# Five RMS norms summed in column groups with a later total, the forget column added with the mask, and a first solve level by transpose

## What is computed

```python
def rmsnorm(x, g):
    y = xf * lax.rsqrt(jnp.mean(xf * xf, axis=-1, keepdims=True) + EPS)
    return (y * g.astype(jnp.float32)).astype(x.dtype)
...
def fox_attention(q, k, v, logf):
    c = jnp.cumsum(logf, axis=1).transpose(0, 2, 1)
        s = (jnp.einsum("bhqd,bhkd->bhqk", qh[:, :, lo:hi], kh[:, :, :hi]).astype(jnp.float32) * scale
             + (c[:, :, lo:hi, None] - c[:, :, None, :hi]))
        mask = jnp.arange(hi)[None, :] <= jnp.arange(lo, hi)[:, None]
        p = jax.nn.softmax(jnp.where(mask, s, -jnp.inf), axis=-1).astype(vh.dtype)
...
def gated_delta_rule(q, k, v, g, beta):
    sol = lax.linalg.triangular_solve(a_mat, rhs, left_side=True, lower=True)
```

## Time and profile before

| what | value |
|---|---|
| median of 3 runs | 1651.2 us (1650.48 to 1651.35) |
| profiled execution | 1650.75 us, its span 1649.0 us |
| PE busy | 1345.0 us, 82% of the span |
| DVE, ACT busy | 643.2 us (39%), 489.4 us (30%) |
| DMA | 517.93 MB, mean 314 GB/s |
| chain of waits | PE 45%, DMA 42%, DVE 8%, ACT 3% |

### The profile page before, as it was taken

One profiled execution on the slowest core, in us unless ns is written; L12 is line 12 of the kernel. 1 busy time (PEld: TensorE's weight loads), 2 busy tenths in 40 slices (PEclk: granted clock), 3 DMA queues, 4 the chain that ended last, 5 costly groups with the idle time before them and its releaser, 6 DMA issues.

```text
span 1649.0 us, 32820 instructions
## 1 busy us (share of the span) xinstructions
PE 1345.0 (82%) x14402; PEld 1069.4 (65%) x14402; DVE 643.2 (39%) x1008; ACT 489.4 (30%) x819; POOL 0.2 (0%) x4
## 2 busy tenths in 40 slices
PE   9999999999999999998875766676576676668556
PEld 8898899999999999995543433343343343334333
DVE  7787736878887778652110101100010110111001
ACT  6765477456644555531100000000000000000001
POOL 0000000000000000000000000000000000000000
PEclk9999999999999999999998988988898899899889
DMA  8432033553556665489999999999999999999997
GB/s 321 161 128 103 26 129 106 180 201 128 194 179 231 259 226 196 156 350 387 429 428 433 430 427 428 432 430 425 433 426 430 433 429 428 428 430 431 428 432 312
DMA packets 41401, 517.93 MB, mean 314 GB/s; under 512 B 4720, under 2 KB 4848, under 8 KB 6384
## 3 DMA queue, kind: packets, MB, share of 16 engines
q1 hardware_dynamic: 41184, 516.71, 76.5%
q10 hardware_dynamic: 144, 0.17, 0.0%
HBM read 515.81 MB, written 1.05 MB: 313 GB/s over the span
## 4 chain that ended last, share of the span: by engine, by line
PE 45%; DMA 42%; DVE 8%; ACT 3%; issue 1%; SPq 1%; another core or an unknown queue 0%; DVEq 0%; ACTq 0%; PEldq 0%
DMA e_gu<-experts 41%; PE psum L323 9%; PE psum L324 9%; PE psum L325 9%; PE psum L894 7%; PE psum L935 3%; DVE w_low L1562 2%; DVE all_sq L1516 1%; PE psum L385 1%; PE psum L544 1%; ACT w_high L1008 1%; DMA w_raw<-dense 1%; PE psum L941 1%; PE psum L905 0%; DVE a_gdn_qk L1607 0%
## 5 line engine op out<-in xcount | busy, mean ns | idle before, releaser
L894 PE MATMUL psum<-e_gu,x_xt 128*32 128x256 f32 x3072 | 217.2, 446 | 177.9 <-DMA e_gu<-experts 177.8
L894 PEld LDWEIGHTS psum<-e_gu,x_xt 128*32 128x32 f32 x3072 | 108.3, 128 | 279.7 <-DMA e_gu<-experts 188.9
L323 PE MATMUL psum<-h_high,w_high 128*128 128x256 f32 x896 | 254.6, 284 | 2.6 <-DVE w_low L1562 2.6
L324 PE MATMUL psum<-h_low,w_high 128*128 128x256 f32 x896 | 251.7, 281 | 0.0
L325 PE MATMUL psum<-h_high,w_low 128*128 128x256 f32 x896 | 251.6, 281 | 0.0
L1562 DVE TENSOR_TENSOR w_low<-w_raw,w_high 128x2048 fp32r<-128x2048 f32 x100 | 228.4, 2288 | 46.5 <-ACT w_high L1008 41.6
L1008 ACT ACTIVATE w_high<-w_raw 128x2048 fp32r<-128x2048 f32 x100 | 191.2, 1914 | 64.8 <-PE psum L325 53.1
L2213 DVE COPY x_yb<-psum 128x256 f32<-128x256 f32 x64 | 27.2, 425 | 427.3 <-PE psum L935 427.3
L323 PEld LDWEIGHTS psum<-h_high,w_high 128*128 128x128 f32 x896 | 168.8, 188 | 3.7 <-DVE w_low L1562 3.2
L324 PEld LDWEIGHTS psum<-h_low,w_high 128*128 128x128 f32 x896 | 168.9, 188 | 0.4 <-issue 0.2
L325 PEld LDWEIGHTS psum<-h_high,w_low 128*128 128x128 f32 x896 | 168.8, 188 | 0.0
(11 more groups left out here) (447 smaller groups left out, 2145.4 us busy)
## 6 DMA issues: line engine op xcount, KB each, us to landing
e_gu<-experts SPq DMA_DIRECT2D x44, 4096.0 KB, 53.0
w_raw<-dense SPq DMA_DIRECT2D x100, 1024.0 KB, 4.8
e_dn<-experts SPq DMA_DIRECT2D x46, 2048.0 KB, 49.4
e_dn<-experts SPq DMA_DIRECT2D x36, 1024.0 KB, 54.8
e_gu_lo<-experts SPq DMA_DIRECT2D x16, 2048.0 KB, 51.5
e_gu_hi<-experts SPq DMA_DIRECT2D x16, 2048.0 KB, 55.9
e_gu<-experts SPq DMA_DIRECT2D x8, 1024.0 KB, 8.1
e_gu<-experts SPq DMA_DIRECT2D x2, 2560.0 KB, 10.3
```

What stands on the lines that cost most here:

```text
L323: mm(ps, w[0], src[0], start=start, stop=False, **kw)
L324: mm(ps, w[0], src[1], start=False, stop=False, **kw)
L894: last = mm(half(psum[32 * s:32 * s + 32, GU_BANK[j % 2], 0:256], P), X["xt"][:, k, CAP * j:CAP * (j + 1)], expert_gu(j, k)[:, :, s * P:(s ...
```

## The change

The five norms mix, mem, xq, ffn and n1 sum in two steps. `group_sums` makes eight products with 32 columns of ones; chunk k goes to the column group k mod 4, so that two chunks are added in each quarter of a bank's partitions. ScalarE copies the result to `sq[:, 1, :]` (`keep_sums`). `total` sums the copy over all partitions with one full-width product by ones into the other half of the bank, and ScalarE takes the root with the scale 1/(32 x 1024) (`mean_root`). For mix the total follows the group sums at once; for mem, xq and n1 it stands in the middle of the next unit; for ffn behind the rest of U0. On ScalarE the high parts of weights change places with the root: in mix three of them go behind it, and in xq and n1 one does.

The product that added c of the query goes; `tok_c` turns c into a column for each head instead (two products behind fv1, copied by VectorE), and VectorE adds column and mask in one instruction for each block of queries. Level 0 of the solve uses TensorE's transpose.

```diff
-            def mean_square(name, first=0, last=DC):
...
-                    ins = mm(ps[:, 0:T], C("inv1024"), sq[:, k, :], start=(k == 0), stop=(k == DC - 1))
...
+            def group_sums(name):
+
+                ps = aux.fill(pe, f"ms_{name}")
+                for k in range(DC):
+                    pe.wait_ge(sem("squares"), quarter(name, k // 2))
+                    g = 32 * (k % 4)
+                    ins = mm(ps[g:g + 32, 0:T], C("ones", n=32), sq[:, k, :], start=(k < 4), stop=(k >= 4))
+                ins.then_inc(sem("group_sums"), 1)
+
+            def total(name):
+
+                pe.wait_ge(sem("group_sums_kept"), NORMS.index(name) + 1)
+                ps = psum[:, aux.banks[aux.units[f"ms_{name}"] % len(aux.banks)], :]
+                aux.filled(mm(ps[:, T:2 * T], C("ones", n=P), sq[:, 1, :], start=True, stop=True), f"ms_{name}")
...
-            mean_square("mix")
+            group_sums("mix")
+            total("mix")
...
+            def tok_c():
+
+                ps = aux.fill(pe, "tok_c")
+                for t in range(TT):
+                    last = mm(ps[:, t * H:(t + 1) * H], A["rows"][0:H, 3, t * P:(t + 1) * P], ident[0:H, 0:H],
+                              start=True, stop=True)
+                aux.filled(last, "tok_c")
...
+            pe.wait_ge(sem("fox_c"), 1)
+            tok_c()
             head_sums("fss_q", "fox_sq", lambda hd: sq[:, hd, :], T)
...
-                    mm(o, C("negsel", H, hd * P, P), cs[:, 0:n], start=False, stop=False)
-                    last = mm(o, cs[:, t * P:(t + 1) * P], C("sel", H, hd * 256, n), start=False, stop=True)
+                    last = mm(o, C("negsel", H, hd * P, P), cs[:, 0:n], start=False, stop=True)
...
+                    if lv == 0:
+                        last = nc.tensor.transpose(o, A["lm"][:, un, :], ident)
...
-            mean_square("mem")
-            unit("out10", mixed); unit("out11", mixed)
+            group_sums("mem")
+            unit("out10", mixed, between=lambda: total("mem")); unit("out11", mixed)
             unit("mk0", hm, split_input("mem"))
-            mean_square("xq")
-            unit("mk1", hm)
+            group_sums("xq")
+            unit("mk1", hm, between=lambda: total("xq"))
...
                 proj.filled(last, f"up{c}")
+                if c == 0:
+                    total("ffn")
...
-            mean_square("n1")
-            unit("q21", r_gained)
+            group_sums("n1")
+            unit("q21", r_gained, between=lambda: total("n1"))
...
             squares("mix", x, lambda q: (sem(f"x_loaded{q // 2}"), 16))
+            keep_sums("mix")
+            act.wait_ge(sem("consts_loaded"), 16)
+            mean_root("mix")
             ahead(UNITS[0], 2)
-            act.wait_ge(sem("consts_loaded"), 16)
-            root("ms_mix", sq[:, 0, :])
             ahead(UNITS[0], 3)
...
             warm(ACT.Sqrt)
-            root("ms_mem", sq[:, 0, :])
+            keep_sums("mem")
             ahead("out01")
+            mean_root("mem")
...
             warm(ACT.Sqrt)
-            root("ms_ffn", sq[:, 0, :])
+            keep_sums("ffn")
+            mean_root("ffn")
...
+            warm(ACT.Sqrt)
             turn_raw("q", 0)
+            keep_sums("n1")
+            mean_root("n1")
             ahead("q20")
-            warm(ACT.Sqrt)
-            root("ms_n1", sq[:, 0, :])
...
+            ps = aux.wait(dve, "tok_c")
+            aux.emptied(V.tensor_copy(A["tok"][:, :, 20:24], half(ps[:, 0:8], 4)), "tok_c")
             lows("sq1")
...
-                link(V.tensor_copy(s, ps[:, 0:n]) if mask is None else V.tensor_tensor(s, ps[:, 0:n], mask, ALU.add))
+                for t, (lo, w) in enumerate(spans):
+                    c = slice(lo, lo + w)
+                    last = V.scalar_tensor_tensor(s[:, c], ps[:, c], row(t), mask[:, c], ALU.add, ALU.add)
+                link(last)
```

More of the change, by code:

```diff
@@ L341, in chunk_ready, with unit @@
                     pe.wait_ge(sem(ready[0]), seen[0])
-            def unit(name, src=HI, ready=None, order=range(DC), by_chunk=False):
+            def unit(name, src=HI, ready=None, order=range(DC), by_chunk=False, between=None):
                 w, seen = parts(name, DC), [0]
@@ L347, in unit @@
                 for k, i in [(k, i) for k in order for i in range(2)] if by_chunk else [(k, i) for i in range(2) for k in order]:
+                    if between and (k, i) == (order[0], 1):
+                        between()
                     chunk_ready(ready, k, seen)
@@ L378, in unit_o @@
                 done[name] = proj.full(f"{tile}{u}")
-            def mean_square(name, first=0, last=DC):
-                ps = aux.fill(pe, f"ms_{name}") if first == 0 else psum[:, 4 + aux.units[f"ms_{name}"] % 4, :]
-                for k in range(first, last):
+            def group_sums(name):
+                ps = aux.fill(pe, f"ms_{name}")
+                for k in range(DC):
                     pe.wait_ge(sem("squares"), quarter(name, k // 2))
-                    ins = mm(ps[:, 0:T], C("inv1024"), sq[:, k, :], start=(k == 0), stop=(k == DC - 1))
-                if last == DC:
-                    aux.filled(ins, f"ms_{name}")
+                    g = 32 * (k % 4)
[5 more added lines that the diff above has]
+                aux.filled(mm(ps[:, T:2 * T], C("ones", n=P), sq[:, 1, :], start=True, stop=True), f"ms_{name}")
             def head_sums(name, ready, src, width, weights="inv128", heads=range(H), counted=0):
@@ L527, in solve_x @@
                     un = t * H + hd
-                    last = mm(ps[:, hd * P:(hd + 1) * P], A["lm"][:, un, :], ident if lv == 0 else A["t"][:, un, :],
-                              start=True, stop=True)
+                    o = ps[:, hd * P:(hd + 1) * P]
+                    if lv == 0:
+                        last = nc.tensor.transpose(o, A["lm"][:, un, :], ident)
+                    else:
+                        last = mm(o, A["lm"][:, un, :], A["t"][:, un, :], start=True, stop=True)
                 aux.filled(last, f"x{lv}{t}")
@@ L980, in root, with keep_sums, mean_root @@
                 act.sem_inc(sem("root_ready"), 1)
+            def keep_sums(name):
+                act.wait_ge(sem("group_sums"), NORMS.index(name) + 1)
+                ps = psum[:, aux.banks[aux.units[f"ms_{name}"] % len(aux.banks)], :]
+                ac(sq[:, 1, :], ps[:, 0:T], ACT.Copy).then_inc(sem("group_sums_kept"), 1)
+            def mean_root(name):
+                act.wait_ge(*aux.full(f"ms_{name}"))
+                ps = psum[:, aux.banks[aux.units[f"ms_{name}"] % len(aux.banks)], :]
+                link(ac(sq[:, 0, :], ps[:, T:2 * T], ACT.Sqrt, scale=1.0 / (32 * D), bias=C("eps")))
+                aux.release(act, f"ms_{name}")
+                act.sem_inc(sem("root_ready"), 1)
             def squares(name, src, ready):
@@ L1276, in mem_keys @@
                 act.sem_inc(sem("mem_sq_k"), 2)
-                ahead(f"mk{u}")
             mem_keys(0)
             warm(ACT.Sqrt)
-            root("ms_xq", sq[:, 0, :])
+            keep_sums("xq")
+            mean_root("xq")
+            ahead("mk0")
             high_parts("xq", M["mem"], h_high)
             mem_keys(1)
+            ahead("mk1")
             for hd in range(H):
```

5 lines of the change are left out of this document (2 added, 3 removed).

## The result

The changed kernel takes **1657.3 us** in the median of five executions (1655.7 to 1660.3); the ratio to the kernel before is 1.0042 (95% interval 1.0031 to 1.0053). It is slower by 0.42%, where I had forecast 1652.8 and no more than 1656.5. The profiled execution took 1655.68 us, 4.93 us more than the profiled one of before.

What follows compares the result with a forecast made beforehand. TensorE's products bound it to 748 us, then expert weight transfers, with dense-part shifts passed on to the end. Terms 4.4 + 0 + 0.2 + 0 − 1.45 − 0.15 + 0.15 − 1.55 = +1.6 gave 1652.8 us, range 1648.5 to 1656.5.

Steps and rivals of the forecast that it cites:

- Clock in the opening: TensorE's idle from 18.1 to 23.1 us may halve the clock for 4.8 us; slack covers it: zero, +2 as other end.
- TensorE waits some 2 us in front of mk0, and so in front of mq0: Sign at mem and xq: TensorE, 2.11 us sooner, waits for low parts; both norms together −0.15 us.
- the wait at 450.34 is over 2 us long: Sign at ffn: the wait of 1.14 us there takes in TensorE's whole saving.
- a sign of being wrong: Expert stage: longer or shorter by over 1 us would be wrong, as nothing in the change touches it.
- The total stands 24 products behind the group sums, so the root is ready 0.73 us later: Norms: −2.54 + 2.84 + 0.43 = 0.73 us later root, where TensorE's sums are what it waits for.
- The opening: Norm mix: VectorE's reciprocal at 25.3 instead of 20.85, gv1's product near 49.8; all reaches TensorE: +4.4 us.
- The forget column, tok_c and the transposes: Mask of four heads −1.45 us; two products behind fv1 +0.2; first solve level as a transpose 0.
- The 32-column sums: Each norm's group sums: 16 records over about 1.07 us, four side by side, ending 2.54 us sooner.
- rival 2: Norms: column groups don't run side by side, root 3.27 us later everywhere: +13.3, 1664.5 us; chance 0.08.
- rivals 3 and 4: Faster: norms hidden, only the opening costs, 1646.3, chance 0.07; only TensorE's work counts, opening hidden too, 1637.3, chance 0.03.
- ffn: Norm ffn: later reciprocal mostly absorbed, leaving +0.15 us; the wait at 450.34 takes TensorE's saving.
- My first rival: Opening: clock at 1.2 GHz for 14 us instead of 4.8, +3.2, 1656 us; chance 0.04.

Runs made afterwards that it cites:

- a4_fox_n1: Kernel before with only the transposes, tok_c, forget column in the mask and n1 changed; mix, mem, xq, ffn old: 1647.73 us, ratio 0.9983.
- a1_mix_back: Changed kernel with the norm mix put back as before, everything else still changed: 1651.19 us, ratio 1.0004.
- a2_mix_only: Kernel before with the norm mix alone changed: 1655.75 us, ratio 1.0032.
- a3_filled: Changed kernel with unused products of ones, ten ahead of gq1 and four each ahead of gv1, mk0 and mq0: 1654.99 us, ratio 1.0026.
- b1_early: Kernel before with transposes, tok_c, forget column, mem, xq, n1 changed, totals placed earlier, mem's root ahead of a weight's high part: 1644.57 us, ratio 0.9965.
- c1_early_filled: b1_early with four unused products of ones ahead of gv1: 1644.80 us, ratio 0.9962.
- c3_mix_order: b1_early with mix's group sums and total too, but ScalarE's old order; total 30 products into gq1: 1646.06 us, ratio 0.9970.
- b2_mem_xq: a4_fox_n1 with mem and xq changed too, exactly as in the change: 1651.37 us, ratio 1.0005.
- c0_gv1_filled: Kernel before with four unused products of ones ahead of gv1: 1649.91 us, ratio 0.9995.

## Why the prediction was wrong

**The clock, the largest miss: +3.1 us in the profiled execution.** The step that failed is "Clock in the opening": I asked about the clock only behind the 5 us idle, because the earlier trace rows show it there. That part was right: the clock fell at 22.9, and the slack took it (5.4 us late in the middle of gq1, 4.56 at gk1). What I had not asked is what waits of 1.8 to 2 us do, though my own text forecast that the change would make new ones ("TensorE waits some 2 us in front of mk0, and so in front of mq0"; "the wait at 450.34 is over 2 us long"). I took such a wait to be free where TensorE's saved work had made it. It isn't: a low stretch of 3.4 us can follow, with 1.5 to 1.6 us of products lost at gv1 and mq0 and no slack behind. The Trainium skill ("TensorE: Matmul & The Clock Gate", "Why this matters for your kernels"), which I had quoted for the opening, warns of idle gaps between bursts of matmuls, but of longer ones than these waits. Here the measurement differs and decides: low stretches stand at 50.2 and 381.3 us, behind waits of 1.83 and 2.04 us.

**The profile of one execution hid it.** The profiled execution of before passed its wait of 1.83 us at 45.40 at full clock; by the two groups, it costs 1.4 us in 40 of 75 executions. Its expert stage, last product to the end of the span, took 912.3 us, against 911.1 to 912.1 in the thirteen other traces; that is the -1.12 us in the last row of the table. I had named a shift of over 1 us there as a sign of being wrong, and it came. The kernel before has the longest of the fourteen, by 0.2 us, and no kernel differs in this stage, so I take it for the spread between executions; what sets that spread isn't shown. I had set 1650.75 against 1651.2 as if the two differed by chance alone.

**The total's price, +1.2 us over three norms.** The step is "The total stands 24 products behind the group sums, so the root is ready 0.73 us later". Measured at mem it is 4.60 - 3.66 = 0.94, and the low part of mk0 is 1.06 later relative to the rest. I had counted the group sums with the time to their last result (1.07 includes it) and the total with its two issue distances only (0.43), where it takes 0.60 to its end. mk0 then starts 0.06 after its low part: +0.28 instead of -0.10. xq repeats it, +0.47 instead of -0.05, and n1 gains 1.24 instead of 1.55: 0.38, 0.52 and 0.31 more than my terms. The mechanism was right: TensorE waits 1.93 and 2.04 us there.

**The opening was right**: reciprocal at 25.41 (I said 25.3), gv1 4.56 later at 49.97 (I said 4.4 and 49.8). **The forget column, tok_c and the transposes** gave 1.33 us in `a4_fox_n1` and 1.60 in the changed kernel, for 1.25. sq0 is 1.27 us later (I said 1.1) and has all but 0.16 back by 134 us (I kept 0.2). The transposes start the next products 0.9 sooner, and the rest of level 0 takes that and the 0.16 back. Heads 0 and 1 give 1.36 (I said 1.26). Heads 2 and 3 give nothing in `a1_mix_back` and `a4_fox_n1`; the 0.24 of the changed kernel stands with 0.20 in `a2_mix_only` too, which has no forget column in the mask, so it isn't theirs (I said 0.2). **The 32-column sums** take 1.07 us and run side by side, so rival 2 is out; rivals 3 and 4 are, by the new waits at 364.63 and 379.92. **ffn** cost 0.08, for 0.15: the root ends 1.6 us after the copy starts, as I had it, and the wait at 457.63 takes in what is left of TensorE's saving; it is 1.78 us long, where I had said over 2.

**The sum again**: 1.6 + 3.1 (clock) + 0.16 + 0.9 + 0.31 (opening, mem and xq, n1) + 0.38 (pause) - 0.07 (ffn) - 0.35 (solve) - 1.1 (experts) = 4.9, as measured. The median stands 1.6 us above the profiled execution, whose four fellows took 1656.5 to 1660.3. I have no trace of them; that they have more low stretches, say behind the wait of 1.78 us at 457.63, which passed at full clock in the profile and not in `a3_filled`, fits but isn't shown. The ratio's 0.42% is 6.9 us and the medians differ by 6.1; the two traces account for 4.9. My first rival gave 1656 by low clock, but in the opening and 14 us long; the place was wrong and so was the length, 3.4 us. What rival and forecast both lacked was a term for low clock behind each wait.

**The best version** is `b1_early`, with `c1_early_filled` equal to it: 0.35% faster than the kernel before and 0.77% faster than the changed one (0.9965 against 1.0042). It keeps the old mix and ffn, and takes the parts that gain, with the total as soon as the copy of the group sums is ready.

## What to carry to other kernels

A reduction split in two steps is worth its saved time only where its second step is issued as soon as the first is copied: in the middle of the next unit, 24 products on, the root came 0.9 us later than with one slow step, 9 products on 0.9 us sooner (3.66 us from the first sum to the root before, 4.60 and 2.80 with group sums). Before moving an instruction on a helper engine (ScalarE's root ahead of three high parts), ask which engine is the next to starve: 4.6 us came of an order in which the sum itself was faster. And price a new wait of TensorE not only by its length but also by the clock of what follows it; where executions of a kernel fall in two groups, look for such a wait.

## What the runs showed of the hardware

**Low clock follows waits, not always.** Fourteen traces (all that are told of here) have 17 low stretches before 745 us, of 3.4 us, two of them 6.8. Each begins between 1.1 us before and 1.4 us after the end of a wait of TensorE that is in the table; none stands anywhere else. What TensorE did before, and how often a low stretch followed:

| wait of TensorE | followed by 0.50 |
|---|---|
| 5.04 to 5.06 us, ahead of gq1 | 3 of 3 |
| 2.81 us, ahead of gk0 (`c3_mix_order`) | 1 of 1 |
| 2.35 and 2.58 us, in gq0 | 2 of 2 |
| 1.06 to 2.04 us, in gq0 | 0 of 12 |
| 2.04 us, ahead of mq0 | 3 of 3 |
| 1.93 and 1.94 us, ahead of mk0, 15 us earlier | 0 of 3 |
| 1.83 to 1.85 us, ahead of gv1 | 4 of 7 |
| 0.90 to 1.54 us, ahead of gv1 | 0 of 3 |
| 1.77 to 1.79 us, ahead of a down unit | 2 of 4 |
| 1.35 and 0.91 us, 1.4 us apart, in the solve | 2 of 10 |
| 1.13 to 1.23 us, at 310 and 450 us | 0 of 24 |

The same wait with the same work around it is followed by low clock in one execution and not in the next (gv1: yes in `a4_fox_n1` and `b1_early`, no in `b2_mem_xq`), so a single profile does not tell what a wait costs. Two of them, with what was granted in the executions that were profiled; first `b2_mem_xq` through gv1's wait, then `a4_fox_n1`:

```profile
45.30:48.70 3.40, 3.40 (x29) 3.40 (x30) 3.18 (x7) 0.82 (x1) 0.00 (x0) 1.00 0.66 272
```

```profile
45.70:49.10 3.40, 3.40 (x19) 3.40 (x18) 3.18 (x6) 0.46 (x1) 0.00 (x0) 0.50 0.57 239
```

29 products start in one and 19 in the other. With eight records of products of ones in gv1's wait (1.89 us), no low stretch followed in four traces of four, and they cost nothing in `c0_gv1_filled`, as they stand where TensorE was idle.

**A pause of VectorE that goes with its own code.** VectorE's step after its addition at 422.6 follows 0.24 us behind it in the kernel before and 0.60 in the changed one (429.44 and 0.69 long, then 430.73):

```profile
423.52 1.67 DVE L1545 SCALAR_TENSOR_TENSOR f_gained_low<-all_x,all_sm,f_gained_high 128x256 fp32r<-128x256 f32 x4 [0.24 <-DVE all_x L1868]
```

```profile
430.73 1.67 DVE L1586 SCALAR_TENSOR_TENSOR f_gained_low<-all_x,all_sm,f_gained_high 128x256 fp32r<-128x256 f32 x4 [0.60 <-DVE all_x L1915]
```

It is 0.24 or 0.25 in the four traces without tok_c and the two-part mask, and 0.60 in all ten with them, at starts from 419.6 to 430.7 us. TensorE had come to this point with no slack, and pays 0.36. The step itself is the same in all fourteen; what they have in common is how many instructions VectorE has behind it. Why it pauses just there isn't shown.
